# A third pair of PSUM banks in the token mixers, the gated unit earlier in the order, the S5 set-up later, and head sums carried into the head norm

## What is computed

```python
for l in range(2):
    h = rms_norm(x, mix_norm[l])
    u, q, k, v, g_ssm, g_attn = split(h @ w_in[l])           # 512, 1024, 1024, 1024, 1024, 1024
    y_a = gelu(s5_branch(u))                                  # diagonal state space model
    y_a = y_a * sigmoid(y_a @ w_glu[l] + b_glu[l])            # the gated unit
    # differential attention, 8 heads, two maps each, 128-wide values
    w = softmax(q1 k1) - lam * softmax(q2 k2)
    o = w @ v
    y_b = rms_norm(o, subln[l], 1e-5) * (1 - lam_init)        # the head norm
    m = sigmoid(g_ssm) * (y_a @ w_proj_ssm[l]) + sigmoid(g_attn) * (y_b @ w_proj_attn[l])
    x = x + m @ w_out[l]
    x = x + ffn(rms_norm(x, ffn_norm[l]))                     # layer 0 dense, layer 1 top-2 of 8 experts
```

## Time and profile before

| | us |
|---|---|
| median of three runs | 1610.73 |
| the profiled execution, its own time | 1613.62 |
| span of its trace | 1611.9 |
| TensorE (PE) busy | 1508.3 |
| DVE busy | 1239.2 |
| ACT busy | 915.1 |

### The profile page before, as it was taken

One profiled execution on the slowest core, in us unless ns is written; L12 is line 12 of the kernel. 1 busy time (PEld: TensorE's weight loads), 2 busy tenths in 40 slices (PEclk: granted clock), 3 DMA queues, 4 the chain that ended last, 5 costly groups with the idle time before them and its releaser, 6 DMA issues.

```text
span 1611.9 us, 23240 instructions
## 1 busy us (share of the span) xinstructions
PE 1508.3 (94%) x8684; PEld 1268.0 (79%) x8684; DVE 1239.2 (77%) x1408; ACT 915.1 (57%) x952; POOL 25.3 (2%) x60
## 2 busy tenths in 40 slices
PE   5799889899997999987799999999999999999996
PEld 5688777789997887775688888888888888888885
DVE  5988775484455697764798988989889898898986
ACT  5144553433343345633477767767677676676764
POOL 0000000000000000100000000000000000000000
PEclk9799999899998999998899999999999999999998
DMA  6254335344453443343599897998989989899893
GB/s 231 92 166 158 118 107 203 138 147 177 141 185 153 169 149 125 123 152 111 206 365 352 319 362 306 374 352 308 369 308 370 356 313 360 315 357 359 325 353 142
DMA packets 76638, 391.49 MB, mean 243 GB/s; under 512 B 28320, under 2 KB 28448, under 8 KB 29728
## 3 DMA queue, kind: packets, MB, share of 16 engines
q1 hardware_dynamic: 74960, 389.71, 64.6%
q10 hardware_dynamic: 1616, 0.92, 0.2%
HBM read 386.80 MB, written 1.05 MB: 241 GB/s over the span
## 4 chain that ended last, share of the span: by engine, by line
PE 78%; DVE 9%; ACT 4%; issue 3%; SPq 2%; DMA 2%; POOL 0%; DVEq 0%; ACTq 0%; POOLq 0%
PE psum L1609 24%; PE psum L1610 23%; PE psum L1611 23%; DVE w_lo L530 3%; PE psum L1625 3%; ACT w_hi L524 3%; SPq L612 2%; DMA w_raw<-in_stream 2%; PE psum L1881 1%; DVE hsT_lo L1165 1%; PE psum L1650 1%; ACT prob L892 1%; PE psum L1897 1%; PE psum L1898 1%; PE psum L1713 1%
## 5 line engine op out<-in xcount | busy, mean ns | idle before, releaser
L530 DVE TENSOR_TENSOR w_lo<-w_raw,w_hi 128x2048 fp32r<-128x2048 f32 x270 | 614.2, 2288 | 199.2 <-ACT w_hi L524 196.7
L524 ACT ACTIVATE w_hi<-w_raw 128x2048 fp32r<-128x2048 f32 x270 | 513.7, 1912 | 310.7 <-PE psum L1611 270.5
L1609 PE MATMUL psum<-w_hi,hsT_hi 128*128 128x512 f32 (+1 forms) x512 | 190.3, 372 | 6.3 <-issue 6.3
L1610 PE MATMUL psum<-w_hi,hsT_lo 128*128 128x512 f32 (+1 forms) x512 | 189.4, 370 | 0.0
L1611 PE MATMUL psum<-w_lo,hsT_hi 128*128 128x512 f32 (+1 forms) x512 | 188.2, 368 | 0.0
L1609 PE MATMUL psum<-w_hi,hT_hi 128*128 128x512 f32 x384 | 157.1, 409 | 8.9 <-ACT gate_attn L839 6.9
L1611 PE MATMUL psum<-w_lo,hT_hi 128*128 128x512 f32 x384 | 152.6, 397 | 0.0
L1610 PE MATMUL psum<-w_hi,hT_lo 128*128 128x512 f32 x384 | 152.4, 397 | 0.0
L530 DVE TENSOR_TENSOR w_lo_more<-w_raw,w_hi_more 128x2048 fp32r<-128x2048 f32 x56 | 128.0, 2286 | 23.5 <-ACT w_hi_more L524 23.5
L1609 PE MATMUL psum<-hT_hi,w_hi 128*128 128x256 f32 x416 | 120.4, 289 | 0.9 <-DVE act_ff L1388 0.9
L1610 PE MATMUL psum<-hT_hi,w_lo 128*128 128x256 f32 x416 | 119.6, 288 | 0.0
(11 more groups left out here) (365 smaller groups left out, 2753.9 us busy)
## 6 DMA issues: line engine op xcount, KB each, us to landing
w_raw<-in_stream SPq DMA_DIRECT2D x326, 1024.0 KB, 6.1
w_raw_more<-in_stream SPq DMA_DIRECT2D x40, 1024.0 KB, 7.1
x_tok<-in_x SPq DMA_DIRECT2D x1, 1024.0 KB, 5.3
uT_lags<-uT_by_lag SPq DMA_DIRECT2D x64, 16.0 KB, 1.9
zT_by_lag<-uT_lags SPq DMA_DIRECT2D x64, 16.0 KB, 1.9
out_trunk<-out_tok SPq DMA_DIRECT2D x2, 512.0 KB, 2.7
s_direct<-s_direct_lags SPq DMA_DIRECT2D x40, 16.0 KB, 2.3
s_b_raw<-in_s_b SPq DMA_DIRECT2D x2, 256.0 KB, 6.2
```

The lines of the kernel that those rows point to most:

```text
L524: nc.scalar.activation(split_of(seg, i)[0], raw_of(seg, i), ACT.Copy).then_inc(s_hi, 1)
L530: nc.vector.tensor_tensor(l_, raw_of(seg, i), h.bitcast(F32), ALU.subtract).then_inc(s_lo, 1)
L1609: mm(out, lh, rh, start=start, stop=False)
L1610: mm(out, ll, rh, start=False, stop=False)
```

## The change

The reads of z and the gated unit move from slot 22 to slot 20; the second attention gate block (now GA1, block 11) follows it; banks 6 and 7 become a third pair (number 3), which block 9 takes once the last S5 output has been read. The projections of the S5 branch and of the attention alternate in another order. `z_from_lags` stands behind the load of slot 21. The S5 set-up products of layer 0 move two slots later, and DVE's powers are cut in halves over four steps. In the FFN they do so too, over j = 1 to 4, the set-up products stand at j = 4 and 6, and `shift_direct` of layer 1 stands behind the load of slot 26, not 22. In the heads the first map is no longer scaled: the sum of its exponentials is carried into the factor of the second map and, squared, into the epsilon of the head norm.

```diff
-U_BLOCK, GLU, PS0, PA0, WO0 = 0, 11, 12, 13, 16
-PAIR_OF = [0, 1, 0, 1, 0, 1, 0, 0, 0, 0, 0, 0, 0, 1, 0, 1, 0, 1]
-LATE_SLOTS = [(11, 0, 1), (13, 0, 2), (12, 0, 1), (13, 1, 2), (14, 0, 1), (15, 0, 2), (15, 1, 2),
-              (16, 0, 2), (17, 0, 2), (16, 1, 2), (17, 1, 2)]
+U_BLOCK, GLU, GA1, PS0, PA0, WO0 = 0, 10, 11, 12, 14, 16
+PAIR_OF = [0, 1, 0, 1, 0, 1, 0, 0, 0, 3, 0, 3, 0, 3, 1, 0, 3, 1]
+LATE_SLOTS = [(GLU, 0, 1), (GA1, 0, 2), (GA1, 1, 2), (PS0, 0, 1), (PA0, 0, 2), (PS0 + 1, 0, 1), (PA0, 1, 2),
+              (PA0 + 1, 0, 2), (PA0 + 1, 1, 2), (WO0, 0, 2), (WO0 + 1, 0, 2), (WO0, 1, 2), (WO0 + 1, 1, 2)]
...
-SETUP_MID = {3: [("bT", 2), ("bT", 3)]}
-SETUP_TAIL = {2: [("bT", 0), ("bT", 1)], 3: [("tT", 0)]}
-FFN_SETUP = {3: ([("bT", 0), ("bT", 1)], [("bT", 2), ("bT", 3)]), 4: ([("tT", 0)], [])}
+SETUP_MID = {5: [("bT", 2), ("bT", 3)]}
+SETUP_TAIL = {4: [("bT", 0), ("bT", 1)], 5: [("tT", 0)]}
+FFN_SETUP = {4: ([("bT", 0), ("bT", 1)], [("bT", 2), ("bT", 3)]), 6: ([("tT", 0)], [])}
...
+    if s == 30:
+        todo.append(("mT", 1))
...
-    if s in (27, 29):
-        todo.append(("mT", (s - 27) // 2))
+    if s == 27:
+        todo.append(("mT", 0))
...
-                    if (seg, i) in ((0, 11), (1, 22)):
+                    if (seg, i) in ((0, 11), (1, 26)):
                         shift_direct(seg)
...
-                    if seg != 1 and i == 22:
+                    if seg != 1 and i == 21:
                         z_from_lags(seg // 2)
...
-                        rms_power(HEADS * l + s - 16, oms, oss, ors, 2, 1.0 / P, SUB_EPS, s_osq, s_ors)
+                        h = s - 17
+                        pool.wait_ge(s_osq, HEADS * l + h + 1)
+                        own.do(nc.gpsimd.tensor_tensor(oms[:, :], oss[:, :], oeps[:, 2 * (h % 2):2 * (h % 2) + 2], ALU.add))
+                        own.settle()
+                        nc.gpsimd.tensor_tensor(ors[:, :], oms[:, :], mhalf[:, 0:2], ALU.pow).then_inc(s_ors, 1)
...
-                    if s == 23:
+                    if s == 21:
                         for c in range(CT):
...
-                    if s in (16, 18, 20, 22):
+                    if s in (16, 18, 20, 23):
...
+                    if s == 22:
+                        act.wait_ge(s_yg, l + 1)
+                        nc.scalar.activation(by_block(ySh), by_lag(zT), ACT.Copy, scale=0.25).then_inc(s_ygh, 1)
...
-                        own.do(V.reciprocal(rs[:, :], sm[:, :]))
+                        own.do(V.reciprocal(rs[:, 0:2], sm[:, 1:4:2]))
+                        own.do(V.scalar_tensor_tensor(oeps[:, 2 * (h % 2):2 * (h % 2) + 2], sm[:, 0:4:2], SUB_EPS, sm[:, 0:4:2],
+                                                      ALU.mult, ALU.mult))
                         own.settle()
-                        own.do(V.tensor_scalar(c2[:, :], rs[:, 1:4:2], nlam[:, l:l + 1], None, ALU.mult))
+                        own.do(V.scalar_tensor_tensor(c2[:, :], rs[:, 0:2], nlam[:, l:l + 1], sm[:, 0:4:2], ALU.mult, ALU.mult))
                         own.settle()
                         for q in range(NT):
                             sl = slice(q * P, q * P + (q + 1) * P)
-                            own.do(V.tensor_scalar(prob[:, 1, sl], prob[:, 1, sl], c2[:, q:q + 1], None, ALU.mult))
-                        own.settle()
-                        for q in range(NT):
-                            sl = slice(q * P, q * P + (q + 1) * P)
-                            i = V.scalar_tensor_tensor(prob[:, 0, sl], prob[:, 0, sl], rs[:, 2 * q:2 * q + 1],
-                                                       prob[:, 1, sl], ALU.mult, ALU.add)
+                            i = V.scalar_tensor_tensor(prob[:, 0, sl], prob[:, 1, sl], c2[:, q:q + 1],
+                                                       prob[:, 0, sl], ALU.mult, ALU.add)
...
-                    if l == 0 and s < 3:
+                    if l == 0 and s < 5:
                         split_ahead(dve_split, dve, seg, s)
...
                     if l == 0 and s == 1:
-                        b_powers(0)
+                        b_powers(0, 0)
                     if l == 0 and s == 2:
-                        c_powers(0)
+                        b_powers(0, 1)
+                    if l == 0 and s in (2, 3):
+                        c_powers(0, s - 2)
...
+                    if s == 22:
                         dve.wait_ge(s_ygh, 2 * (l + 1))
                         V.scalar_tensor_tensor(by_block(ySl), by_lag(zT), 0.25, by_block(ySh).bitcast(F32), ALU.mult,
                                                ALU.subtract).then_inc(s_ygl, 1)
...
+                    if l or s >= 5:
+                        split_ahead(dve_split, dve, seg, s)
+                    if s == 21:
+                        dve.wait_ge(s_accA, ACCA_L * l + 2 * sum(1 for k in range(GLU + 1) if k in EVAC_BY_ACT))
+                        V.scalar_tensor_tensor(by_lag(zT), by_block(glt), 1.0, by_lag(zT), ALU.add, ALU.mult).then_inc(s_yg, 1)
+                    if s in (24, 26, 27, 29, 32):
+                        out_block(l, {24: PS0, 26: PS0 + 1, 27: PA0, 29: PA0 + 1, 32: WO0}[s])
+                    if s in (27, 29):
...
-                        if j == 1:
-                            b_powers(1)
-                        if j == 2:
-                            c_powers(1)
-                        if j == 3:
+                        if j in (1, 2):
+                            b_powers(1, j - 1)
+                        if j in (3, 4):
+                            c_powers(1, j - 3)
+                        if j == 4:
                             start_turns(own, 1)
...
+                        if blk == 9:
+
+                            pe.wait_ge(s_yv, QUADS * (l + 1))
```

More of the change, by code:

```diff
@@ L74 @@
 Z_LANDED_AT = 19
[L77 to L79 removed]
+SETUP_MID = {5: [("bT", 2), ("bT", 3)]}
+SETUP_TAIL = {4: [("bT", 0), ("bT", 1)], 5: [("tT", 0)]}
+FFN_SETUP = {4: ([("bT", 0), ("bT", 1)], [("bT", 2), ("bT", 3)]), 6: ([("tT", 0)], [])}
 def block_column(b):
[L84 removed]
+    return (b - PS0 if b < PA0 else b - PA0 if b < WO0 else b - WO0) * 512
 def lam_init(l):
@@ L838, in _ @@
                             act.wait_ge(s_acc, 2 * (B0 + b) + q + 1)
-                            nc.scalar.activation(dst[:, q, ((b - 7) % 2) * 512:((b - 7) % 2 + 1) * 512],
-                                                 bank(q), ACT.Tanh, scale=0.5).then_inc(s_accA, 1)
+                            nc.scalar.activation(dst[:, q, col * 512:(col + 1) * 512],
+                                                 bank(2 * PAIR_OF[b] + q), ACT.Tanh, scale=0.5).then_inc(s_accA, 1)
                     if 0 <= s - 18 < HEADS:
@@ L895, in _ @@
                         i.then_inc(s_ex, 1)
-                    if s == 23:
-                        act.wait_ge(s_yg, l + 1)
-                        nc.scalar.activation(by_block(ySh), by_lag(zT), ACT.Copy, scale=0.25).then_inc(s_ygh, 1)
                     if s in (28, 30):
@@ L1112, in constants, with b_powers @@
                 own.settle()
-            def b_powers(l):
-                dve.wait_ge(s_b, 16 * (l + 1))
+            def b_powers(l, part):
+                if part == 0:
+                    dve.wait_ge(s_b, 16 * (l + 1))
                 ls = slice(l * PAIRS, (l + 1) * PAIRS)
@@ L1121, in b_powers @@
                 x1, x2 = pw1[:, :, :, :], pw2[:, :, :, :]
-                own.do(V.tensor_tensor(x1, br, gr, ALU.mult))
-                own.do(V.tensor_tensor(x2, bi, gi, ALU.mult))
-                own.settle()
-                V.tensor_tensor(Bl[l][:, 0], x1, x2, ALU.subtract).then_inc(s_bl, 1)
-                dve.wait_ge(s_bl, 2 * l + 1)
+                if part == 0:
+                    own.do(V.tensor_tensor(x1, br, gr, ALU.mult))
+                    own.do(V.tensor_tensor(x2, bi, gi, ALU.mult))
+                    own.settle()
+                    V.tensor_tensor(Bl[l][:, 0], x1, x2, ALU.subtract).then_inc(s_bl, 1)
+                    dve.wait_ge(s_bl, 2 * l + 1)
+                    return
                 own.do(V.tensor_tensor(x1, br, gi, ALU.mult))
@@ L1147, in c_powers @@
                           for c in range(2))
-                own.do(V.tensor_tensor(x1, cr, pr, ALU.mult))
-                own.do(V.tensor_tensor(x2, ci, pi, ALU.mult))
-                own.settle()
-                own.do(V.tensor_tensor(Ere[:, :, 1:LAGS + 1, :], x1, x2, ALU.subtract))
-                own.settle()
+                if part == 0:
+                    own.do(V.tensor_tensor(x1, cr, pr, ALU.mult))
+                    own.do(V.tensor_tensor(x2, ci, pi, ALU.mult))
+                    own.settle()
+                    own.do(V.tensor_tensor(Ere[:, :, 1:LAGS + 1, :], x1, x2, ALU.subtract))
+                    own.settle()
+                    return
                 own.do(V.tensor_tensor(x1, cr, pi, ALU.mult))
@@ L1242, in out_block @@
                     if b < WO0:
-                        g_ = gs if b in (PS0, PS0 + 2) else ga
+                        g_ = gs if b < PA0 else ga
```

(9 more changed lines are left out.)

53 lines of the change are left out of this document (20 added, 33 removed).

## The result

The kernel after takes 1573.03 us (median of four runs, 1572.00 to 1574.63), the kernel before 1610.05 (four runs, 1608.73 to 1611.67): ratio 0.9774, 95% interval 0.9759 to 0.9790, that is 37.0 us less. The forecast was 1586.2 with a range from 1578: the sign was right, and 12.5 us more were won than forecast. The profiled execution took 1574.63, its span 1572.9.

The account below looks back on a forecast made before the run. TensorE was taken as the bound (78% of the chain of waits), so only its waits and low clock counted. Gains 19.2 + 3.3 + 2.0 = 24.5 us take 1610.73 to 1586.2; range 1578 to 1594, with the first two rivals to 1600.

Parts of the forecast that it names:

- start: Layer 0 set-up products two slots later: TensorE's first product after the rope earlier; 2.0 us gained, bounds -2 to 4.2.
- mixers: Both layers: TensorE waits and low clock of 28.8 us fall to 9.6, a gain of 19.2 us.
- FFN: Powers cut in four remove 3.2 us of waits and 1.7 of clock, against 1.6 of new wait: gain 3.3.
- The wait is 0.6 a layer: Slot 20, gated unit: with z's copies 3.7 us earlier, TensorE still waits 0.6 us a layer for yS_lo.
- 1.8 to 1.9: DVE's spare us per head step, including shorter head arithmetic, against 2.0 us of added work in steps 21 and 22.
- the 8.9 us for the clock: Four half-clock stretches behind the layer gates and before PS0: 1.65 + 1.65 + 2.87 + 2.75 us lost.
- new wait of 1.6: Near the FFN's end, later shift_direct delays load 27; TensorE waits 1.6 us, bounds 0 and 4 with the clock.
- 1.70 lost: FFN, behind the 2.4 us wait at j = 2: TensorE ran 3.40 us at half clock; this loss was to go.
- wait for the rope: Start: TensorE reaches the transposes by about 76 us, idles some 5 us; then low clock for 4 to 6 us.
- (1): Head phase: new waits replace the old, DVE and ACT become the bound; 10.5 us lost, time 1597, chance 0.22.
- (2): z is no earlier, so the gated unit waits 3.5 us more, plus clock; 11.5 us lost, 1598, chance 0.05.
- (3): Slots 20 to 22: clock stays low through the head phase; 40 us in both layers, 1626, slower, chance 0.04.

Follow-up runs that it names:

- tile alone: Kernel before plus only the unused 32-byte tile o_eps, moving every address behind it by 32 bytes: 1599.55 us, ratio 0.9959 to before.
- both with 64 more: 64 bytes left free behind o_eps: kernel before with that tile added 1593.85 us (ratio 0.9915), kernel after 1567.87 us (0.9753).
- the tile last: Kernel after with o_eps allocated behind all other tiles, so every address is that of the kernel before: 1583.27 us, ratio 0.9857.
- the best kernel: Kernel after with the last turn doublings behind the rope, first-half transposes of m in slot 28, and 64 bytes free behind o_eps: 1560.33 us, ratio 0.9707.

## Why the prediction was right or wrong

| part | forecast | before, after | tile alone, after | both with 64 more |
|---|---|---|---|---|
| start | 2.0 | 2.2 | 0.3 | 1.1 |
| mixers | 19.2 | 22.7 | 22.6 | 20.6 |
| FFN | 3.3 | 5.0 | 3.1 | 3.8 |
| rounds | 0 | 9.1 | -0.1 | 1.4 |
| sum of the traces | 24.5 | 39.0 | 25.9 | 26.7 |

The last two columns compare kernels whose tiles lie alike. There the forecast of 24.5 is right to 1.4 and 2.2 us, and with the old addresses on both sides the medians gave 23.5. Against the tile alone the medians give 25.7 and the ratios 27.2. Part of that is luck: the mixers won more than forecast in both columns, and the FFN and the start came near by other ways than the ones that I wrote down.

**The step that failed** is the sum itself, "19.2 + 3.3 + 2.0 = 24.5 us": it has no term for the tile that the change allocates. I costed each instruction and wait and gave the memory layout nothing, not even as a bound, and none of my rivals stood for it. It is worth 7.2 us on the kernel before; taken from the kernel after it costs 9.5 by the medians and 10.8 by the ratios. The intervals are too wide to tell these apart. Of the 9.1 us in the rounds 8 x 0.88 = 7.0 are the addresses. The rest is late loads in the one trace of before: three of its seven rounds last 101.57, 101.28 and 101.88 us in place of 100.85, 2.2 in all, and in just these three the chain holds a load of over 7 us (start, us; for the first ACT stood 1.5 us):

```profile
1069.37 7.48 DMA w_raw<-in_stream
1271.78 7.16 DMA w_raw<-in_stream
1373.05 7.76 DMA w_raw<-in_stream
```

**Mixers.** "The wait is 0.6 a layer" for yS_lo: 0.81 and 0.82. The copies started at 158.8, 0.03 behind the last product of L1323 as forecast, and ACT took z at 181.6:

```profile
L615 SPq DMA_DIRECT2D zT_by_lag<-uT_lags x32: 594/595/1757, 158.8 to 179.8; - x32
```

```profile
L882 ACT ACTIVATE yS_hi<-zT_by_lag x1: 2062/2062/2062, 181.6 to 181.6; 128x1024 fp32r<-128x1024 f32 x1
```

The weights of head 6 wait 0.32 (forecast 0.5), PS0 1.1 (1.2), head 7 0.75 (1.0), m 1.42 (1.45): 4.4 a layer in place of 4.8, and no clock drop. The spare of "1.8 to 1.9" on DVE against 2.0 was as thin as I said: without the 0.45 of the head sums the weights wait twice as long (2.2 a layer in place of 1.1). But the waits before PS0 become shorter then, so the five together grow only from 4.4 to 4.7 in layer 0 and 5.2 in layer 1. Part of what lacks to the 20.6 is that a wait costs more than its gap: the two of 0.4 for gate_ssm, when gone, gave 0.60 to 0.65 each. And the 8.9 us for the clock were read from one trace: the four stretches of half clock in the head phases last 20 us in all there, 24 with the tile alone and 17 with 64 bytes more, with the same instructions.

**FFN.** 3.3 came out near, by two errors that cancel. The "new wait of 1.6" did not come in the kernel after, but the path to it is there: the copies ended sooner than the 14.04 of the earlier trace rows, which has one slow issue in it, so load 27 was out at 432.7 and landed 5.2 us later, and ACT took it at 438.04, 0.2 after that.

```profile
L624 SPq DMA_DIRECT2D s_direct<-s_direct_lags x20: 591/609/614, 419.7 to 432.0; - x20
```

With the tile last the load comes late, ACT stands for it and TensorE waits 0.76 at 445.8; the best kernel has 0.62 at the same place:

```profile
440.86 1.92 ACT L527 ACTIVATE w_hi<-w_raw 128x2048 fp32r<-128x2048 f32 x1 [5.22 <-DMA w_raw<-in_stream]
```

And the "1.70 lost" to the clock did not go: the kernel after has 3.3 us of half clock behind tT. That the drop of before came from the wait of 2.4 was my reading of one trace; the run with the FFN undone and the kernel before with 64 bytes more have that wait and no drop behind it, so the wait alone does not bring it. What decides between the two places is open.

**Start.** 2.0 forecast, 0.3 to 2.2 between traces, 1.3 by the run that undoes it. The wait for the rope is there, 5.4 us, and the low clock lasts 5 us beyond it, as forecast. But the waits did not become fewer, because those of 5.9 and 1.9 for w_lo are new and stood nowhere in the forecast: between 30 and 90 us TensorE's waits are 14.0 us before and 14.8 after. What was won is clock: TensorE was busy at 1.2 GHz for 3.96 + 12.81 = 16.8 us before and for 3.21 + 3.40 + 4.94 = 11.6 after, and half of the difference, an estimate of what that gives back, is 2.6.

**Rivals.** (1) did not happen, not even in the run without the sums, where the weights wait twice as long and the clock stays at 1.00 in both head phases. (2) was priced right (11.5; 12.0 when made true). (3), the clock low through the head phase, did not happen: four short waits within 30 us and the clock at 1.00. The rule of the Trainium skill beside it, page "TensorE: Matmul & The Clock Gate", section "A second HAM failure mode: psum-queue depth-cycling", did not show here.

## What to carry to other kernels

Before a change is costed, list what it allocates and where: a tile of 32 bytes in the middle of a list moved everything behind it, and that was worth a third or more of the intended gain, here by luck in the right direction. Give the large operands of TensorE their places first (for the 512-wide products here the same place against 256 bytes was best) and the small tiles the places behind them, and compare two versions only where their tiles lie alike. And where an engine is busy without a pause ahead of another's wait, look for work in that stretch that is first needed much later; moving it gave more than the start's whole part here.

## What the runs showed of the hardware

The interval of 128x512 fp32 matmuls depends on how the two operands stand to each other in a partition: for w_lo_more with eactT_hi it is 227.2 ns with 0 bytes between them beyond a multiple of 256, 232.1 with 128 and 233.8 with 96. For 256-wide ones the order is another: 113 to 114 with 64, 118 to 122 with 0, 96 or 128. Over the whole kernel the layouts tried on the kernel before are worth 7.2 and 13.2 us of 1607. Why it is so was not tried, nor products of other types.

The granted clock fell to 0.50 for 3.3 us behind the small set-up products tT (3.8 us), at 419.3 after and at 389.7 with the FFN undone, though TensorE had no gap there. In the trace of before the same products are followed by no such stretch, and with 64 bytes more and the same instructions they are.
